# A hybrid mixer block on one core: the third attention's values projected with the steps and forget gates, its keys projected once

## What is computed

```python
proj = h @ w_in
(m_z, m_xbc, m_dt, b_qkv, c_qkv, c_f, d_q, d_kv, gate_logits) = jnp.split(proj, SPLIT_POINTS, axis=-1)
...
dk, dv = jnp.split(d_kv, 2, axis=-1)          # 128 columns each: 2 heads of 64
y_d = sliding_window_attention(heads(d_q, N_HEADS), heads(dk, SWA_KV_HEADS), heads(dv, SWA_KV_HEADS),
                               sinks, rel_bias[:, N_HEADS:])
branches = jnp.stack([y_a, y_b, y_c, y_d], axis=2)
branch_out = jnp.einsum('bsiw,iwd->bsid', branches, w_branch)
gates = jax.nn.sigmoid(gate_logits.reshape(bsz, s_len, N_BRANCHES, D_MODEL))
return jnp.sum(gates * branch_out, axis=2) @ w_out
```

## Time and profile before

| | us |
|---|---|
| median of 3 runs | 1179.19 |
| lowest and highest of them | 1178.02, 1179.58 |
| the profiled execution's own time | 1177.87 |
| its span, first to last instruction | 1176.6 |
| PE busy in the span | 1142.4 (97%) |
| DVE busy | 670.1 (57%) |
| ACT busy | 583.0 (50%) |
| POOL busy | 295.9 (25%) |
| mean granted clock of PE | 0.989 |

### The profile page before, as it was taken

The page is one execution under the profiler, slowest core; times in us unless marked ns, Lnnn a source line. Parts: engine busy times, 40 slices in busy tenths (PEclk is TensorE's granted clock), DMA queues, the critical chain, the costliest instruction groups (busy, mean ns, idle before and its releaser), DMA issues.

```text
span 1176.6 us, 19533 instructions
## 1 busy us (share of the span) xinstructions
PE 1142.4 (97%) x8221; PEld 1061.1 (90%) x8221; DVE 670.1 (57%) x1043; ACT 583.0 (50%) x891; POOL 295.9 (25%) x191
## 2 busy tenths in 40 slices
PE   8999999999999999999899999999999869999997
PEld 6999989999989999889898889999889858999986
DVE  6555765577656454337897556334247785533424
ACT  6546555555436644337543444444345954544432
POOL 2023100000005444512321115444500001544440
PEclk9899999999999999999999999999999989999999
DMA  8669574545646666655443447655555534756550
GB/s 261 203 206 331 151 242 125 165 144 144 205 148 194 189 191 203 197 162 179 143 150 107 125 153 226 192 184 195 197 161 169 172 96 144 226 180 193 184 195 36
DMA packets 158257, 207.89 MB, mean 177 GB/s; under 512 B 13631, under 2 KB 131545, under 8 KB 158170
## 3 DMA queue, kind: packets, MB, share of 16 engines
q1 hardware_dynamic: 154442, 193.63, 52.8%
q0 software_dynamic: 3728, 13.02, 3.3%
HBM read 205.53 MB, written 4.24 MB: 178 GB/s over the span
## 4 chain that ended last, share of the span: by engine, by line
PE 88%; DVE 6%; ACT 3%; issue 1%; DMA 1%; POOL 0%; SPq 0%; DVEq 0%; ACTq 0%; POOLq 0%
PE bank L495 18%; PE bank L501 18%; PE bank L498 18%; PE bank L518 9%; PE bank L515 9%; PE bank L512 9%; DVE wlo L1369 2%; PE bank L857 2%; ACT whi L958 1%; PE bank L783 1%; PE bank L793 1%; DMA area<-in_hgrn_lb 1%; PE bank L805 1%; PE bank L558 1%; DVE uc L1499 0%
## 5 line engine op out<-in xcount | busy, mean ns | idle before, releaser
L1369 DVE TENSOR_TENSOR wlo<-raw,whi 128x1024 fp32r<-128x1024 f32 (+1 forms) x281 | 346.1, 1260 | 236.1 <-ACT whi L958 235.5
L958 ACT ACTIVATE whi<-raw 128x1024 fp32r<-128x1024 f32 x368 | 365.6, 1042 | 118.2 <-PE bank L518 112.6
L495 PE MATMUL bank<-hh,whi 128*128 128x256 f32 x1792 | 287.1, 281 | 1.7 <-ACT hh L990 1.7
L1942 POOL TENSOR_TENSOR wlo<-raw,whi 128x1024 fp32r<-128x1024 f32 x87 | 223.3, 2567 | 255.9 <-ACT whi L958 255.9
L501 PE MATMUL bank<-hl,whi 128*128 128x256 f32 x1792 | 282.6, 279 | 0.0
L498 PE MATMUL bank<-hh,wlo 128*128 128x256 f32 x1792 | 282.6, 279 | 0.0
L495 PEld LDWEIGHTS bank<-hh,whi 128*128 128x128 f32 x1792 | 242.4, 188 | 6.7 <-issue 5.5
L498 PEld LDWEIGHTS bank<-hh,wlo 128*128 128x128 f32 x1792 | 241.7, 188 | 0.0
L501 PEld LDWEIGHTS bank<-hl,whi 128*128 128x128 f32 x1792 | 241.7, 188 | 0.0
L1949 POOL TENSOR_TENSOR st<-st,half 128x1 f32<-128x1 f32 x18 | 10.3, 581 | 438.3 <-DVE st L1386 413.4
L512 PE MATMUL bank<-whi,gh 128*128 128x512 f32 x264 | 81.5, 390 | 0.0
(11 more groups left out here) (306 smaller groups left out, 1281.1 us busy)
## 6 DMA issues: line engine op xcount, KB each, us to landing
raw<-in_ffn_w_in SPq DMA_DIRECT2D x88, 512.0 KB, 3.6
raw<-in_w_in SPq DMA_DIRECT2D x72, 512.0 KB, 4.7
raw<-in_ffn_w_out SPq DMA_DIRECT2D x44, 512.0 KB, 3.4
raw<-in_hgrn_w_in SPq DMA_DIRECT2D x32, 512.0 KB, 4.3
raw<-in_w_ffn_gate SPq DMA_DIRECT2D x22, 512.0 KB, 4.4
raw<-in_w_ffn_up SPq DMA_DIRECT2D x22, 512.0 KB, 4.1
raw<-in_w_ffn_down SPq DMA_DIRECT2D x22, 512.0 KB, 3.3
raw<-in_w_branch SPq DMA_DIRECT2D x16, 512.0 KB, 4.3
```

What stands on the lines that cost most here:

```text
L495: T.matmul(out, wh[:, i, c], xh[:, k, :], start=first and (i, k) == pairs[0], stop=False)
L958: A.activation(half_of(whi, j, h), half_of(raw, j, h), ACT.Copy).then_inc(s_hi[j % NS][h], 1)
L1369: V.tensor_tensor(half_of(wlo, j, h), half_of(raw, j, h), half_of(whi, j, h).bitcast(f32), ALU.subtract).then_inc(s_lo[j % NS][h], 1)
L1942: G.tensor_tensor(half_of(wlo, j, 1), half_of(raw, j, 1), half_of(whi, j, 1).bitcast(f32), ALU.subtract).then_inc(s_lo[j % NS][1], 1)
```

## The change

The unit `dtf` gets a third piece, the 128 value columns of the third attention, and is 144 columns wide. Its 48 matmuls have 144 columns in place of 16. DVE copies the values out of the bank into a tile `dv` of their own before the steps are taken. The unit `dv` and its fill go. The unit `dk` is 128 columns wide, with each key column once, and `project_columns` runs one tile of 128 in place of two for it. ACT writes the two key heads from the bank, head 0 to the lower rows and head 1 to the upper rows, and two transfers that POOL starts copy each to the other half of the rows. The third attention's first scores wait for both copies (`s_dk`).

```diff
         unit(("dtf",), [(0, 8, w_in[:, 1536:1544].rearrange("(c p) n -> p c n", p=128)),
-                        (8, 8, w_in[:, 4616:4624].rearrange("(c p) n -> p c n", p=128))], 8, 16)
+                        (8, 8, w_in[:, 4616:4624].rearrange("(c p) n -> p c n", p=128)),
+                        (16, 128, w_in[:, 5264:5392].rearrange("(c p) n -> p c n", p=128))], 8, 144)
...
-        unit(("dk",), [(64 * j, 64, w_in[:, 5136 + (j // 2) * 64:5200 + (j // 2) * 64].rearrange("(c p) n -> p c n", p=128))
-                       for j in range(4)], 8, 256)
-        cols(("dv",), w_in, 5264, 128)
+        cols(("dk",), w_in, 5136, 128)
...
-                 ([("d", 1)], [("dk",), ("dv",)]), ([("br", 1, 0)], [("br", 1, 1)]), ([("gate", 2, 0)], [("gate", 2, 1)]),
+                 ([("d", 1)], [("dk",)]), ([("br", 1, 0)], [("br", 1, 1)]), ([("gate", 2, 0)], [("gate", 2, 1)]),
...
-                for m in range(2):
+                for m in range(units[j][2] // 128):
                     t = still(banks[b][:, 256 * m:256 * m + 256], j, m, hh, hl, range(8), *of_norm(e))
...
-                tok = moving(banks[b][:, 16 * t:16 * t + 16], j, t, hh, hl, range(8), 0, 16, *of_norm(0))
+                tok = moving(banks[b][:, 144 * t:144 * t + 144], j, t, hh, hl, range(8), 0, 144, *of_norm(0))
...
+                    if n == 3:
+                        tq.wait_ge(s_dk, 32)
...
                 elif what[0] == "dk":
-                    columns(what, dk[:, 0:2, :], ACT.Copy)
-                elif what[0] == "dv":
                     use(what)
-                    aq.wait_ge(*full("dv"))
-                    A.activation(dv[:, :, 0:128], bank_of("dv")[:, 0:256].rearrange("p (t n) -> p t n", n=128),
-                                 ACT.Copy).then_inc(evacuated("dv"), 1)
+                    b = bank_of("col", *what)
+                    aq.wait_ge(*full("col", *what))
+                    A.activation(dk[0:64, 0, :], b[0:64, 0:256], ACT.Copy)
+                    A.activation(dk[64:128, 1, :], b[64:128, 0:256], ACT.Copy).then_inc(evacuated("col", *what), 1)
...
-            V.tensor_tensor(y0, bank_of("dtf")[:, 0:32].rearrange("p (t n) -> p t n", n=16), bias16, ALU.add).then_inc(evacuated("dtf"), 1)
+            dtf_bank = bank_of("dtf")[:, 0:288].rearrange("p (t n) -> p t n", n=144)
+            V.tensor_copy(dv[:, :, :], dtf_bank[:, :, 16:144])
+            V.tensor_tensor(y0, dtf_bank[:, :, 0:16], bias16, ALU.add).then_inc(evacuated("dtf"), 1)
...
+                    gq.wait_ge(*evac("col", *what))
+                    G.dma_start(dk[64:128, 0, :], dk[0:64, 0, :]).then_inc(s_dk, 16)
+                    G.dma_start(dk[0:64, 1, :], dk[64:128, 1, :]).then_inc(s_dk, 16)
```

More of the change, by code:

```diff
@@ L124, in build @@
         prow = sbuf(mix, "prow", [128, 40])
+        dv = sbuf(mix, "dv", [128, 2, 128])
         mix.close()
@@ L201, in build @@
         bq, bk, bv = qkv(area)
-        dq, dk, dv = qkv(qkv0)
+        dq, dk, _ = qkv(qkv0)
         units = []
@@ L337, in build @@
         s_nm, s_pe, s_pn = sem("score_max_set"), sem("probabilities_set"), sem("probabilities_normed")
-        s_acc = sem("acc_added")
+        s_acc, s_dk = sem("acc_added"), sem("keys_doubled")
         s_silu, s_gh, s_gl = sem("silu_set"), sem("gh_set"), sem("gl_set")
@@ L522, in of_norm, with project_columns @@
                 return (lambda k: hh_set(e, k)), (lambda k: hl_set(e, k))
-            def project_columns(key, e, tiles=2):
+            def project_columns(key, e):
                 j = unit_at[key]
@@ L766, in tensor_program @@
                       2: [("col", "b", j) for j in range(4)] + [("tok", "bv", t) for t in range(2)],
-                      3: [("col", "d", 0), ("col", "d", 1), ("col", "dk"), ("dv",)]}
+                      3: [("col", "d", 0), ("col", "d", 1), ("dtf",)]}
             def scores(n, hp):
@@ L2027, in fill @@
                         G.dma_start(dst, src).then_inc(s_w, 16)
+                elif what[0] == "dk":
+                    gq.wait_ge(*evac("col", *what))
+                    G.dma_start(dk[64:128, 0, :], dk[0:64, 0, :]).then_inc(s_dk, 16)
+                    G.dma_start(dk[0:64, 1, :], dk[64:128, 1, :]).then_inc(s_dk, 16)
                 else:
```

## The result

The changed kernel takes 1167.02 us (median of 4 runs, 1166.40 to 1169.06) against 1179.16 us: a ratio of 0.990, 95% interval 0.988 to 0.992. The forecast was 1167.9 us, and the range 1165.1 to 1171.3. The profiled execution took 1169.06 us (span 1167.8), the longest of the four. That it agrees is not yet a reason: three terms were added up, and each has to be found in the trace.

A forecast was written before the change was run, and what follows sets the result against it. PE, busy 97% of the span, was taken to bound the kernel; 2.82 (keys) + 5.35 (values) + 3.13 (clock) = 11.30 us less gave 1167.9 us against the median 1179.19, range 1165.1 to 1171.3.

The forecast's parts named there:

- three terms: Keys in turn 6 2.82 us less, the values' own unit 5.35 less, the clock at the head 3.13 less.
- the sum: Whole kernel: 2.82 + 5.35 + 3.13 = 11.30 us less.
- Turn 6: PE's `dk` loses 24 matmuls, 2.82 us, and `dv` its 48, 5.35 us: together 8.17 us less.
- The wide unit at the price of 0.1119 us a matmul: `dtf` at the head: 48 matmuls of 144 columns take 5.37 us, priced as 128-column ones.
- the row with almost the same shape: Profile row of 128-column matmuls at 0.1119 us each, taken as the price for `dtf` at 144 columns.
- The lower end: Lowest price for the wide `dtf`: 0.10 us a matmul as at 16 columns, 4.9 us for 48.
- The clock: Head, `dtf` and `z`'s first 12 matmuls: clock holds, 3.13 us less; rival that it stays low, 1171.0 us, chance 0.12.
- Work beside PE: Head: ACT 0.87 us and DVE about 1 us more, delaying `z`'s second unit up to 1 us; just covered, costing nothing.
- The transfers of the wide unit: Head: two more issues by SP, last landing at 29.8, covered by 1.1 us or more.
- The copies: Keys' copies land by 224.4, or 230.9 at worst; PE reaches the third attention's scores at 232.0; cost nothing.
- The position of the scores behind `dk`: PE's timeline in turn 6: these scores start 11.3 us before 229.57, at 218.3.
- The rest of the kernel: From the third attention's scores to the end: same work, no cost, 1.5 us either way for clock and spread.

The follow-up runs named there:

- the wide unit alone: Against the kernel before, only `dtf` made 144 columns wide, extra results unused and nothing removed: 1175.78 us, ratio 0.9969.
- the 80 columns: Against the kernel before, `dtf` given 64 extra columns, making 80, with nothing removed: 1179.33 us, ratio 0.9991.
- the values alone: Against the changed kernel, `dk` back at 256 columns without copies or their wait, only the values' move kept: 1170.03 us, ratio 0.9912 to the kernel before.
- the keys alone: Against the kernel before, only `dk` cut to 128 columns with two copies and the new wait; `dv` stays: 1177.90 us, ratio 0.9986.
- the keys late: Against the changed kernel, `dk` projected one turn later, directly ahead of the third attention's first scores: 1176.25 us against 1168.02.

## Why the prediction was right

The table above gives the balance. Means of three profiles before and four after: start 37.46 and 37.62, to `z` 11.23 and 8.16, to the third scores 195.44 and 187.20, rest 933.6 and 933.7. The span shrinks by 1177.7 - 1166.7 = 11.0 us, where the sum said 11.30. The medians fell by more: 12.1, 11.7, 11.9 and 12.9 us in the four sets of runs. Over all runs, 49 before and 17 changed, the means are 12.2 us apart, give or take 0.7.

- **Turn 6, forecast 8.17 us** (`dk` 2.82, `dv` 5.35): 195.44 - 187.20 = 8.24, of which 0.1 is the clock's part in the third profile of before. Done singly they gave 2.7 and 5.2. Right.
- **The wide unit at the price of 0.1119 us a matmul:** 0.112. Right; the row with almost the same shape was the one to take. The lower end, 0.10 for 16 columns, was misread from the first eight alone. The next two groups at full clock, in the kernel before, are these:

```profile
38.54 1.04 PE L518 MATMUL bank<-whi,hl 128*128 128x16 f32 x8
39.43 1.04 PE L512 MATMUL bank<-whi,hh 128*128 128x16 f32 x8
```

From 37.65 to 39.43 that is 1.78 us for 16 matmuls, 0.111 each: 16 columns cost what 144 do, so the extra columns were free, and not only cheap.

- **The clock, forecast 3.13 us:** 11.23 - 8.16 = 3.07 in the profiles. That the width brings it is shown by the wide unit alone and by the 80 columns. Its size in the times is less sure: the wide unit alone was 4.0 us quicker than before by the medians, the values alone 9.7 where I had 8.5, and the profile with the keys alone has 4.8 us of it. I had read the size from one execution, and the low stretch does not last equally long in all. This is the term that my sum may have made too small, by about 1 us, and it would answer for what the times fell beyond the sum. That is argued, not shown: the three profiles of before do not contain a longer stretch, the intervals of the wide unit alone (2.4 to 5.0 us) and of the change (10.0 to 13.8) take in my 3.1 and 11.3, and the spreads tell little (22 runs of before lie within 6.0 us, 17 of the changed kernel within 4.9).
- **Work beside PE, at nothing:** right for each. ACT's and DVE's extra time was as worked out. `z`'s second unit was ready at 47.87 (forecast 47.7) and had 2.0 us to spare where I counted 1.0. PE began `dtf` 1.11 us later in this profile. ACT was 0.70 later already at the row ahead of its part of `dtf` (31.08 against 30.38) and 1.17 later at `z` (44.44 against 43.27), so the added work delayed `z` by only 0.5 us, where I had counted up to 1. The transfers of the wide unit ended no wait.
- **The copies, at nothing:** right; they landed 7.8 us ahead of PE where I had 232.0 - 224.4 = 7.6. With the keys late the same wait is not covered at all, so that it was free here hangs on turn 7.
- **The position of the scores behind `dk`, forecast 218.3:** it is 219.62. That is 1.3 us off though the terms before it were right. 1.11 us of it is the start of `dtf`, 37.95 against 36.84, and most of what is left is turn 6, which gave 195.19 - 187.27 = 7.92 between these two profiles. The start lies between 35.68 and 39.87 in the profiles of the kernel before alone, before any instruction that the change touches on PE, so the position in one trace against one other was the wrong thing to forecast; the distance from `dtf` was the right one.
- **The rest of the kernel, at nothing within 1.5 us either way:** 933.6 and 933.7 in the mean, 932.8 to 934.4 in single profiles of the changed kernel. Low stretches of the clock come and go there: from 550 to 560 us the changed kernel has a mean of 0.67 to 0.83 in its four profiles, and at the same work, some 10 us later, the kernel before has 0.83 in one profile and 1.00 in two.

## What to carry to other kernels

Matmuls of 16 to 144 columns cost the same here, so columns that a later stage needs can ride along in a unit that is projected anyway, if their result has room until then. Where a busy PE is slow, look at the granted clock and at what PE ran just before it fell: here 48 matmuls of 16 or 80 columns in a row cost more behind them than in them, and filling them up to 144 columns paid with no work removed, to 80 it did not. Before a change is judged by two traces, cut both into pieces between fixed marks, and profile the same kernel twice to learn which pieces move by themselves.

## What the runs showed that I had not expected

**The start of the mixer moves by 4 us.** PE waits near 20 us for a small transfer, for a different time in each run, and in the third profile of before the clock falls behind that wait as well:

```profile
20.26 0.32 PE L660 MATMUL bank<-ident,area 120*128 120x120 f32 x1 [2.58 <-DMA area<-in_hgrn_lb]
```

```profile
20.00:22.00 2.00, 1.74 (x10) 1.74 (x11) 0.44 (x1) 1.34 (x3) 0.00 (x0) 0.67 0.97 320
```

In the second profile it is:

```profile
18.03 0.33 PE L660 MATMUL bank<-ident,area 120*128 120x120 f32 x1 [0.24 <-DMA area<-in_hgrn_lb]
```

with the clock at 1.00 behind it; in the third the next window, 22 to 24 us, has 0.50. Between these two profiles the start of `dtf` moves by 4.2 us and the piece with its low clock by 0.24. So this is where most of their difference comes from (3.7 us in the span), and a place to try for the next gain, which no run here does.

The wait's length does not tell whether the clock falls. It fell behind 2.58 us here and behind 1.91 us in the kernel with 80 columns (0.54 from 20 to 22 us). Behind 2.11, 2.16 and 2.18 us, with the keys alone, the values alone and in the changed kernel, it stayed at 1.00. The row and the window with the values alone:

```profile
20.15 0.32 PE L662 MATMUL bank<-ident,area 120*128 120x120 f32 x1 [2.16 <-DMA area<-in_hgrn_lb]
```

```profile
20.00:22.00 2.00, 1.85 (x16) 1.85 (x17) 0.51 (x2) 1.44 (x4) 0.00 (x0) 1.00 1.03 351
```

**One matmul, two paces.** The 256-column matmuls ahead of `dtf`, in the second profile of the kernel before, the granted clock 1.00:

```profile
25.25 0.62 PE L498 MATMUL bank<-hh,wlo 128*128 128x256 f32 x4
...
27.07 0.62 PE L501 MATMUL bank<-hl,whi 128*128 128x256 f32 x4
```

That is (27.07 - 25.25) / 16 = 0.1138 us each. In the third profile the same groups start at 29.03 and 30.91, (30.91 - 29.03) / 16 = 0.1175 us each, also at a clock of 1.00. From these rows to the start of `dtf` it is 35.68 - 25.25 = 10.43 us in one and 39.87 - 29.03 = 10.84 in the other: 0.4 us between two runs of the same program. I have no cause for it.
